# A decoder layer with a streamed mixture of experts: scratch memory shared with early constants, 8 MB of expert weights loaded ahead for items 10 to 13, finer last transfers, and the residual added in the accumulators

## The chip, the cores and the metric

The kernel runs on one core of one Trainium2 chip. The metric is the device time of one execution in microseconds (us), and the lower it is the better. The profile is that of one execution, and its times count from the first instruction of its span.

## The reference, cut to what matters

The layer takes 256 tokens of width 1024. It runs a sparse attention and an RWKV time mixing side by side, then a cross-attention into 256 memory tokens, and last a mixture of 32 experts of which every token takes four. The change lies in the mixture and in the way from the layers before it into it:

```
h = h + concat(o_nsa, o_rwkv) @ w_out
h = h + memory_cross_attention(rms_norm(h), rms_norm(mem), ...)
# mixture of experts on xt = rms_norm(h)
top_v, top_i = top_k(xt @ router_w + router_b, 4);  gate = softmax(top_v)
for every expert e, on the tokens that chose it:
    hb = xt[tok] @ mlp1_w[e] + mlp1_b[e]              # 1024 -> 2048
    hg = min(hb[::2], 7);  hl = clip(hb[1::2], -7, 7)
    yb = (hg * sigmoid(1.702 * hg) * (hl + 1)) @ mlp2_w[e] + mlp2_b[e]
    y[tok] += gate * yb
return h + y
```

All of it is float32. One expert's weights are 128 partitions x 24576 columns, which is 12 MB, and 32 experts have 384 MB. They are read once, so this stream is most of what the kernel moves.

## The kernel before

**Stages.** The kernel first runs the mixers and the cross-attention (called the front here, up to about 430 us of the trace), with a small ring of three weight slots (`wsl`, 1 MB each) that SyncE's queue fills in the order of `JOBS`. Then the router picks the experts, and the mixture runs in **items**: an item is one expert with up to 64 of its tokens. Items 0 to 31 are the experts in order; more would follow if an expert had more tokens than 64, and with these inputs there are none. Items are worked in pairs, of which `item(j, par)` is one; each pair gathers the tokens of both of its experts once.

**An item on TensorE.** `item` in the tensor block does, in this order: the first bias (L922), the first half of the first matrix (`hidden`, n=0, L909), two transposes (L927), its second half (L909), the transposes of the activations (L942), between them the scatter of the item before (`scatter`, L891: it adds gated results into four PSUM banks that stay open over all items), in odd items the gather for the next pair (`gather`, L882), and last the second matrix (L963). VectorE makes the clamps and products (L1455 to L1462) and ScalarE the sigmoid and the copies out of PSUM (L1498).

**Where the weights lie.** The buffer `ring` holds exactly one item: 24576 columns in six **pieces** of 4096 columns, 2 MB each. Pieces 0 to 3 are the first matrix, 4 and 5 the second. TensorE waits for `piece_in_c` ahead of a piece and counts `piece_used` up when it is through with one. SyncE's queue loads piece c of item i (`item`, `piece`, L1981) once piece c of the item that last used this part of the ring has been used:

```
def item(i, e, which=range(PIECES)):
    for c in which:
        sp.wait_ge(sem("piece_used"), i * PIECES + (c + 1 - PIECES))
        piece(e, c)
```

During the front the ring's memory belongs to the RWKV part. It comes free after that, and the six pieces of item 0 are loaded between the jobs of `w_out` and `xq_w`. In four more buffers that the front is through with (`ox`, `mixT`, `vx`, `qx`, 1 MB each) `piece_ahead` (L1992) puts pieces 0 and 1 of item 1. So at the start of the mixture 16 MB lie ready. The queue then goes on in this order: pieces 0 and 1 of item 2 (once item 0 has used them), pieces 2 to 5 of item 1, pieces 2 to 5 of item 2, and from item 3 on piece by piece.

```
for c in range(W1_PIECES):
    sp.wait_ge(sem("piece_used"), c + 1)
    piece(2, c)
item(1, 1, range(W1_PIECES, PIECES))
item(2, 2, range(W1_PIECES, PIECES))
```

**The scratch of the mixture** (clamps, products, selection matrices, biases, `yb`) lies in `wsl`, and the router's tables in `kxT`. So these 3 MB and 1 MB can't hold weights. Some 14 KB a partition of constants and small buffers (masks, vector rows, `dist`, `sc_c`, `xsq`, `xrs` and others) have their own memory, though only the front reads them.

**The end.** After the last item ScalarE copies `yb` out of PSUM in one piece, the last scatter (L891) runs, then VectorE adds the four open banks to the residual `h` (L1486, four instructions one after the other), and SyncE writes each of the four blocks out as it comes (L2028).

## Time and profile before

| | |
|---|---|
| time, median of 3 runs | 1368.34 us (1367.66 to 1369.61) |
| time of the profiled execution | 1367.88 us |
| its span, first to last instruction | 1366.1 us |
| TensorE busy (matmul) | 1258.0 us, 92% |
| VectorE, ScalarE, GpSimd busy | 352.2, 191.9, 43.5 us |
| read from memory | 440.72 MB, mean 323 GB/s over the span |
| mean granted clock of TensorE | 0.982 |

The profiled execution's time is its span and 1.8 us around it. PE stands for TensorE's matmuls, PEld for its weight loads (which overlap them), DVE for VectorE, ACT for ScalarE, SPq for the queue of SyncE, which issues nearly all transfers. A float32 matmul call shows as two records. Pieces of a chain or a timeline are merged groups of instructions with the start and the length of the group. The releaser behind an arrow is what ended a wait.

### The profile page before, as it was taken

Reading aid. Unit: us, or ns where it says so; the run is one execution under the profiler, and the core shown is the slowest. Engines: PE = TensorE matmul, PEld = TensorE weight load, DVE = VectorE, ACT = ScalarE, POOL = GpSimd, SP = SyncE. Lnnn points to the kernel's source line nnn. Section 1 sums busy time; section 2 is a strip of 40 time slices with the busy share of each in tenths; the row PEclk is TensorE's granted clock in tenths of the full one; section 3 lists DMA queues with packets and bytes.
Section 4 is the critical chain, followed back from the end, with each engine's and each line's share of the span. In section 5 each row is a group of like instructions: output and inputs, shape, how many; then the busy total and the mean of one; then the engine's idle time right before and its main releaser. Section 6 shows DMA issues by size and latency. Waiting matters only on the chain.

```text
span 1366.1 us, 19352 instructions
## 1 busy us (share of the span) xinstructions
PE 1258.0 (92%) x7798; PEld 645.7 (47%) x7798; DVE 352.2 (26%) x843; ACT 191.9 (14%) x457; POOL 43.5 (3%) x98
## 2 busy tenths in 40 slices
PE   7999889879898999999989989899998989989897
PEld 6888777758786333333332323333233332323332
DVE  3364642331224421121211212111111211212111
ACT  2242234411231000000000000000000000000000
POOL 7100001100000000000000000000000000000000
PEclk9999989999998999999999999999999999999999
DMA  7454111119631999999999999999999999999996
GB/s 237 124 113 137 64 63 32 33 32 377 238 133 38 384 385 429 428 429 429 427 429 427 429 429 428 428 429 427 429 429 428 428 428 428 429 429 428 428 427 281
DMA packets 75835, 442.44 MB, mean 324 GB/s; under 512 B 18720, under 2 KB 49550, under 8 KB 50958
## 3 DMA queue, kind: packets, MB, share of 16 engines
q1 hardware_dynamic: 75630, 441.26, 79.1%
q8 instruction: 34, 0.56, 0.2%
q0 software_dynamic: 160, 0.52, 0.1%
q14 instruction: 11, 0.09, 0.0%
HBM read 440.72 MB, written 1.05 MB: 323 GB/s over the span
## 4 chain that ended last, share of the span: by engine, by line
DMA 47%; PE 46%; DVE 4%; ACT 1%; issue 1%; POOL 0%; SPq 0%; DVEq 0%; ACTq 0%
DMA sb_ring<-in_mlp_w 47%; PE ps L909 14%; PE ps L359 9%; PE ps L687 6%; PE ps L963 4%; PE ps L558 2%; PE ps L882 1%; PE ps L891 1%; PE ps L720 1%; PE ps L410 1%; PE ps L816 1%; PE ps L922 1%; PE ps L428 1%; ACT sb_ring L1498 1%; DVE sb_qx L1002 0%
## 5 line engine op out<-in xcount | busy, mean ns | idle before, releaser
L909 PE MATMUL ps<-sb_ring,sb_hnT 128*64 128x512 f32 x2016 | 454.9, 598 | 50.3 <-DMA sb_ring<-in_mlp_w 48.8
L909 PEld LDWEIGHTS ps<-sb_ring,sb_hnT 128*64 128x64 f32 x2016 | 135.8, 137 | 346.1 <-issue 247.9
L963 PE MATMUL ps<-sb_ring,sb_hnT 128*64 128x512 f32 x1024 | 229.5, 596 | 0.0
L1455 DVE TENSOR_SCALAR sb_wsl<-ps 128x256 f32<-128x256 f32 x64 | 27.2, 425 | 659.1 <-PE ps L909 659.1
L963 PEld LDWEIGHTS ps<-sb_ring,sb_hnT 128*64 128x64 f32 x1024 | 72.2, 137 | 133.8 <-issue 132.0
L1498 ACT ACTIVATE sb_wsl<-sb_wsl 128x256 f32<-128x256 f32 x64 | 26.6, 416 | 528.2 <-DVE sb_wsl L1455 528.2
L359 PE MATMUL ps<-sb_hnT,sb_wsl 128*128 128x256 f32 x448 | 98.7, 380 | 1.7 <-DVE sb_hnT L1016 0.9
L359 PEld LDWEIGHTS ps<-sb_hnT,sb_wsl 128*128 128x128 f32 x448 | 84.9, 190 | 14.0 <-DVE sb_hnT L1016 1.3
L891 PE MATMUL ps<-sb_wsl 64*128 64x512 f32 x256 | 63.6, 615 | 0.7 <-ACT sb_wsl L1498 0.7
L882 PE MATMUL ps<-sb_wsl,sb_h 128*128 128x128 f32 x512 | 61.7, 281 | 1.6 <-DVE sb_wsl L1338 1.6
L882 PEld LDWEIGHTS ps<-sb_wsl,sb_h 128*128 128x128 f32 x512 | 60.3, 197 | 1.8 <-DVE sb_wsl L1338 1.8
L1498 ACT ACTIVATE sb_wsl<-ps 128x512 f32<-128x512 f32 (+1 forms) x33 | 19.5, 591 | 286.7 <-PE ps L963 268.8
L1498 ACT ACTIVATE sb_hnT<-ps 128x256 f32<-128x256 f32 (+1 forms) x80 | 31.8, 397 | 50.1 <-PE ps L942 47.5
L1430 DVE TENSOR_TENSOR sb_hnT<-ps,sb_vecs 128x512 f32<-128x512 f32 x32 | 20.6, 686 | 69.9 <-PE ps L882 69.9
L942 PEld LDWEIGHTS ps<-sb_ident,sb_hnT 128*128 128x128 f32 x128 | 12.9, 140 | 50.6 <-issue 26.0
L922 PE MATMUL ps<-sb_wsl,sb_hot 32*64 32x512 f32 x256 | 34.8, 613 | 1.4 <-DVE sb_hnT L1430 1.4
L891 PEld LDWEIGHTS ps<-sb_wsl 64*128 64x128 f32 x256 | 22.0, 186 | 21.8 <-issue 20.3
L687 PE MATMUL ps<-sb_wsl,sb_mixT 128*128 128x256 f32 x128 | 28.9, 385 | 1.4 <-DVE sb_mixT L1212 1.4
L687 PE MATMUL ps<-sb_wsl,sb_ox 128*128 128x256 f32 x128 | 29.6, 391 | 0.0
L558 PE MATMUL ps<-sb_ring 64*64 64x64 f32 x768 | 27.9, 234 | 1.8 <-DVE sb_ring L1155 1.3
L687 PE MATMUL ps<-sb_wsl,sb_qx 128*128 128x256 f32 x128 | 28.6, 382 | 0.5 <-ACT sb_qx L1498 0.5
L359 PE MATMUL ps<-sb_ox,sb_wsl 128*128 128x256 f32 x128 | 28.4, 380 | 0.0
(347 smaller groups left out, 965.8 us busy)
## 6 DMA issues: line engine op xcount, KB each, us to landing
sb_ring<-in_mlp_w SPq DMA_DIRECT2D x190, 2048.0 KB, 24.1
sb_wsl<-in_w_in SPq DMA_DIRECT2D x10, 1024.0 KB, 5.9
sb_wsl<-in_xk_w SPq DMA_DIRECT2D x4, 1024.0 KB, 5.1
sb_wsl<-in_xv_w SPq DMA_DIRECT2D x4, 1024.0 KB, 5.3
sb_wsl<-in_xq_w SPq DMA_DIRECT2D x4, 1024.0 KB, 10.3
sb_wsl<-in_xo_w SPq DMA_DIRECT2D x4, 1024.0 KB, 5.2
sb_wsl<-in_w_in SPq DMA_DIRECT2D x8, 256.0 KB, 4.2
sb_wsl<-in_w_out SPq DMA_DIRECT2D x8, 256.0 KB, 4.1
```

Of the source, the lines that this page charges most:

```text
L359: mm = pe.matmul(t[:, g * T:(g + 1) * T], w[:, k, g * P:(g + 1) * P], act[:, k, :], start=k == 0, stop=k == KD - 1)
L410: mm = pe.matmul(t[64 * par:64 * par + 64, b * P:(b + 1) * P], w[:, k, 64 * b:64 * b + 64], hnT[:, k, par:T:2], start=k == 0, stop=k == KD ...
L558: mm = pe.matmul(t[r, n * CH:(n + 1) * CH], BUF[lhs][r, m, :], moving, start=True, stop=True)
L687: mm = pe.matmul(t[:, tt * T:(tt + 1) * T], lhs(k, tt), w[:, k, :], start=k == 0, stop=k == KD - 1)
L882: mm = pe.matmul(psum[:, 4 + k // 4, k % 4 * PAIR:(k % 4 + 1) * PAIR], h[:, tt, k * P:(k + 1) * P], sel[:, tt, :], start=tt == 0, stop=tt ...
L891: mm = pe.matmul(psum[:, 2 * tt + o2, :], selgT[par][r, tt, :], yb[r, :], start=False, stop=False, skip_group_check=True)
L909: mm = pe.matmul(psum[64 * half:64 * half + 64, 4 + n, :], xgT[:, k, SLOTS * par:SLOTS * par + SLOTS], w[:, at + 512 * half:at + 512 * hal ...
L922: pe.matmul(psum[64 * half:64 * half + 64, 4 + n, :], hot[r, :], bias1[r, :], start=True, stop=False)
L963: mm = pe.matmul(psum[64 * o2:64 * o2 + 64, 7, :], actT[:, 2 * n + m, 64 * q:64 * q + 64], ring[:, at + 512 * o2:at + 512 * o2 + 512], sta ...
L1430: dve.tensor_tensor(xgT[:, 4 * n:4 * n + 4, :], view(psum[:, 4 + n, :], 0, 4, PAIR), bcast(g, P, 4, PAIR), ALU.mult).then_inc(sem("slots_i ...
L1455: dve.tensor_scalar(gl[:, n, :], psum[:, 4 + n, 0:256], 7.0, None, ALU.min).then_inc(sem("glu"), 1)
L1498: return act.activation(o, x, func, **kw)
```

## The change

- The constants and buffers of the front that had their own memory move into one buffer `early`, and the scratch and the tables of the mixture take that same buffer once the front is through. The halves of an item (n = 0, 1) now share one set of `gl`, `ll`, `sg`, and VectorE waits for its own last product ahead of writing them again. `bias1` goes to `hn`, the unread output of the squares (`junk`) to `xrs`.
- So `wsl` and `kxT` can take weights: eight buffers of 1 MB are loaded ahead, two for each of four items. They hold piece 0 of items 10, 11, 12 and 13 (before: pieces 0 and 1 of item 1). The two into `wsl` and the one into `qx` wait for the last jobs of `xo_w`.
- The queue's order in the mixture becomes plain: every piece (i, c) follows on the use of (i-1, c). Piece 0 of item 1 comes in two halves of 1 MB, of which the first waits only for the first half of item 0's piece (`half_used`). In items 10 to 13 the queue skips piece 0, and it adds the four missing increments to `piece_in_0` by hand. TensorE's loop is split into items 2 to 9, four items written out, and items 14 to 29.
- The last piece of the last item comes as 1 MB, 0.5 MB and 0.5 MB.
- After item 13 TensorE adds `h` into the four open banks with four matmuls by the identity. At the end ScalarE copies `yb` in two halves of 256 columns, the last scatter runs in two sides, and the four blocks go from PSUM to `h` by copies: two on VectorE, two on ScalarE.
- The table gets two more entries (index of the last item and of the one before it).

```diff
-        masks4 = sb("masks4", 4, CH)
-        dist = sb("dist", T)
-        sc_c = sb("sc_c", TT, 8, 16)
...
+        early = sb("early", 3680)
...
+        aheads = [(view(ox, 0, 2048), mixT[:, :, :].rearrange("p a b -> p (a b)")), (view(vx, 0, 2048), kxT[:, :, :].rearrange("p a b -> p (a b)")),
+                  (view(wsl, 2048, 2048), view(wsl, 4096, 2048)), (view(qx, 0, 2048), view(wsl, 0, 2048))]
+        AHEAD_AT = 10
...
                     if 1024 * (k + 1) % PIECE == 0:
                         mm.then_inc(sem("piece_used"), 1)
+                    elif stage == 0 and n == 0 and k == 1:
+                        mm.then_inc(sem("half_used"), 1)
...
+                            if last and par and n and q:
+                                pe.wait_ge(sem(f"late_in_{m}"), 16)
...
+            for a in range(4):
+                item((AHEAD_AT + a) // 2, a % 2, 1, ahead=a)
+                for bank in range(4) if a == 3 else ():
+                    pe.matmul(psum[:, bank, :], ident[:, :], h[:, bank // 2, bank % 2 * 512:bank % 2 * 512 + 512],
+                              start=False, stop=False, skip_group_check=True)
...
-            pe.wait_ge(sem("y_out"), last_pair * 2 + 3)
-            scatter(1)
+            for side in range(2):
+                pe.wait_ge(sem("y_out"), last_pair * 2 + 3 + side)
+                cols = slice(256 * side, 256 * side + 256)
+                for tt in range(TT):
+                    for o2 in range(2):
+                        r = slice(64 * o2, 64 * o2 + 64)
+                        mm = pe.matmul(psum[:, 2 * tt + o2, cols], selgT[1][r, tt, :], yb[r, cols],
+                                       start=False, stop=False, skip_group_check=True)
+                    if side:
+                        mm.then_inc(sem("scattered"), 1)
...
+                    dve.wait_ge(sem("swiglu"), i * 2 + 1 + n)
...
-            dve.wait_ge(sem("scattered"), last_pair * 2 + 2)
             for tt in range(TT):
-                for o2 in range(2):
-                    cols = h[:, tt, o2 * 512:(o2 + 1) * 512]
-                    link(dve.tensor_tensor(cols, psum[:, 2 * tt + o2, :], cols, ALU.add), "out_ready")
+                dve.wait_ge(sem("scattered"), last_pair * 2 + 2 + tt)
+                dve.tensor_copy(h[:, tt, 0:512], psum[:, 2 * tt, :]).then_inc(sem("out_left"), 1)
...
+            for tt in range(TT):
+                act.wait_ge(sem("scattered"), last_item + 1 + tt)
+                f(h[:, tt, 512:1024], psum[:, 2 * tt + 1, :], ACT.Copy).then_inc(sem("out_right"), 1)
...
+            def piece_ahead(n, half):
+
+                last_use = {(0, 0): ("wout", 3), (2, 0): ("xout", 1), (2, 1): ("xout", 2), (3, 0): ("xout", 3)}
+                if (n, half) == (1, 0):
                     sp.wait_ge(sem("ox"), 8)
+                elif (n, half) in last_use:
+                    sp.wait_ge(sem("tile_ready"), tiles[last_use[n, half]][1] + 1)
+                lo = 2048 * half
+                sp.dma_start(aheads[n][half], a["mlp_w"][AHEAD_AT + n, :, lo:lo + 2048]) \
+                  .then_inc(sem(f"ahead_in_{n}"), 16)
...
-            for c in range(W1_PIECES):
-                sp.wait_ge(sem("piece_used"), c + 1)
-                piece(2, c)
-            item(1, 1, range(W1_PIECES, PIECES))
-            item(2, 2, range(W1_PIECES, PIECES))
-
-            with sp.Fori(3, NE - 1) as i:
+            sp.wait_ge(sem("half_used"), 1)
+            piece(1, 0, at=(0, PIECE // 2))
+            sp.wait_ge(sem("piece_used"), 1)
+            piece(1, 0, at=(PIECE // 2, PIECE))
+            item(1, 1, range(1, PIECES))
+            with sp.Fori(2, AHEAD_AT) as i:
+                item(i, i)
+            for i in range(AHEAD_AT, AHEAD_AT + 4):
+                item(i, i, range(1, PIECES))
+            sp.sem_inc(sem("piece_in_0"), 16 * 4)
+            piece(AHEAD_AT + 4, 0)
+            item(AHEAD_AT + 4, AHEAD_AT + 4, range(1, PIECES))
+            with sp.Fori(AHEAD_AT + 5, NE - 2) as i:
                 item(i, i)
...
+            for c in range(PIECES - 1):
+                sp.wait_ge(sem("piece_used"), before_last * PIECES + (c + 1))
+                piece(e, c)
+            sp.wait_ge(sem("piece_used"), before_last * PIECES + PIECES)
+            piece(e, PIECES - 1, at=(24576 - 4096, 24576 - 2048))
+            piece(e, PIECES - 1, at=(24576 - 2048, 24576 - 1024), name="late_in_0")
+            piece(e, PIECES - 1, at=(24576 - 1024, 24576), name="late_in_1")
```

## Rows read from the trace of the kernel before

**Rows 1.** The page: 40 equal slices of the span, DMA busy tenths and GB/s.

```profile
DMA  7454111119631999999999999999999999999996
GB/s 237 124 113 137 64 63 32 33 32 377 238 133 38 384 385 429 428 429 429 427 429 427 429 429 428 428 429 427 429 429 428 428 428 428 429 429 428 428 427 281
```

**Rows 2.** The chain that ended last, in order of time: start, length, what.

```profile
600.68 7.02 PE ps L909 x32
608.06 7.04 PE ps L909 x32
615.26 24.29 DMA sb_ring<-in_mlp_w
639.60 3.68 PE ps L909 x16
643.43 25.49 DMA sb_ring<-in_mlp_w
...
1319.03 25.49 DMA sb_ring<-in_mlp_w
1344.57 3.65 PE ps L909 x16
```

**Rows 3.** Timeline of TensorE in items 3 to 5: start, length, operation.

```profile
538.81 7.09 PE L963 MATMUL ps<-sb_ring,sb_hnT 128*64 128x512 f32 x32
545.83 1.09 PE L922 MATMUL ps<-sb_wsl,sb_hot 32*64 32x512 f32 x8
...
592.57 7.09 PE L963 MATMUL ps<-sb_ring,sb_hnT 128*64 128x512 f32 x32
```

**Rows 4.** Stretches: start:end, us, busy of each engine, granted clock, DMA share, GB/s.

```profile
445.00:465.00 20.00, 19.66 (x100) 6.34 (x98) 12.83 (x35) 2.36 (x6) 0.00 (x0) 1.00 0.98 419
465.00:497.00 32.00, 32.00 (x168) 12.82 (x166) 6.48 (x18) 2.08 (x5) 0.00 (x0) 1.00 0.85 346
497.00:615.00 118.00, 118.00 (x586) 42.96 (x582) 23.19 (x65) 8.75 (x21) 0.00 (x0) 1.00 1.01 428
560.00:1000.00 440.00, 413.52 (x2030) 149.13 (x2027) 80.39 (x227) 32.34 (x78) 0.00 (x0) 1.00 1.01 428
```

**Rows 5.** Timeline of TensorE in items 0 and 1, where the ring's parts come free.

```profile
439.55 7.09 PE L909 MATMUL ps<-sb_ring,sb_hnT 128*64 128x512 f32 x32
...
471.80 7.09 PE L909 MATMUL ps<-sb_ring,sb_hnT 128*64 128x512 f32 x32
...
481.39 3.74 PE L882 MATMUL ps<-sb_wsl,sb_h 128*128 128x128 f32 x32
485.05 7.09 PE L963 MATMUL ps<-sb_ring,sb_hnT 128*64 128x512 f32 x32
```

**Rows 6.** Timeline of SyncE's queue before the mixture and at its start.

```profile
397.73 0.58 SPq L1992 DMA_DIRECT2D sb_ox<-in_mlp_w  x1
398.35 0.43 SPq L1992 DMA_DIRECT2D sb_mixT<-in_mlp_w  x1
398.82 0.52 SPq L1992 DMA_DIRECT2D sb_vx<-in_mlp_w  x1
420.39 0.33 SPq L1992 DMA_DIRECT2D sb_qx<-in_mlp_w  x1
443.24 172.35 SPq L1981 DMA_DIRECT2D sb_ring<-in_mlp_w  x38
```

**Rows 7.** DMA issues: count, KB each, median us from issue to landing.

```profile
sb_ox<-in_mlp_w SPq DMA_DIRECT2D x1, 1024.0 KB, 7.8
sb_mixT<-in_mlp_w SPq DMA_DIRECT2D x1, 1024.0 KB, 9.6
sb_vx<-in_mlp_w SPq DMA_DIRECT2D x1, 1024.0 KB, 11.8
```

**Rows 8.** Line 1981: issue to landing of the ring's transfers, shortest, median, longest.

```profile
DMA to landing us min/median/max: 7.2/24.1/25.5
```

**Rows 9.** The chain: one matmul call of 128x512 by a 128x128 matrix.

```profile
106.70 0.86 PE ps L446 x2
```

**Rows 10.** Timeline of the end, all engines.

```profile
1350.81 7.26 PE L963 MATMUL ps<-sb_ring,sb_hnT 128*64 128x512 f32 x32
...
1350.91 0.38 ACT L1498 ACTIVATE sb_hnT<-ps 128x256 f32<-128x256 f32 x1 [1.50 <-PE ps L942]
...
1358.10 0.60 ACT L1498 ACTIVATE sb_wsl<-ps 128x512 f32<-128x512 f32 x1 [6.80 <-PE ps L963]
...
1358.75 1.99 PE L891 MATMUL ps<-sb_wsl 64*128 64x512 f32 x8 [0.69 <-ACT sb_wsl L1498]
...
1360.78 2.87 DVE L1486 TENSOR_TENSOR sb_h<-ps,sb_h 128x512 f32<-128x512 f32 x4 [10.68 <-PE ps L891]
1361.50 2.51 SPq L2028 DMA_DIRECT2D out_h<-sb_h  x4
```

More of the change, by code:

```diff
@@ L893, in scatter, with landed, hidden @@
                 mm.then_inc(sem("scattered"), 1)
-            def hidden(i, par, n, first, second):
+            def landed(i, c, stage):
+                loads = i + 1 if c or stage == 0 else i + 2
+                pe.wait_ge(sem(f"piece_in_{c}"), loads * 16)
+            def hidden(i, par, n, stage, ahead):
                 for k in range(KD):
@@ L899, in hidden @@
                     c = at // PIECE
[L900 to L903 removed]
+                    if c == 0 and ahead is not None:
+                        if k == 0:
+                            pe.wait_ge(sem(f"ahead_in_{ahead}"), 32)
+                        w, at = aheads[ahead][k // 2], at % 2048
                     else:
                         if at % PIECE == 0:
[L906 removed]
+                            landed(i, c, stage)
                         w = ring
@@ L913, in hidden, with item @@
                         mm.then_inc(sem("piece_used"), 1)
-            def item(j, par, first=False, second=False, last=False):
+                    elif stage == 0 and n == 0 and k == 1:
+                        mm.then_inc(sem("half_used"), 1)
+            def item(j, par, stage, ahead=None, last=False):
                 i = j * 2 + par
+                first = stage == 0
                 pe.wait_ge(sem("slots_in"), j * 2 + 2)
@@ L922, in item @@
                     pe.matmul(psum[64 * half:64 * half + 64, 4 + n, :], hot[r, :], bias1[r, :], start=True, stop=False)
-                hidden(i, par, 0, first, second)
+                hidden(i, par, 0, stage, ahead)
                 pe.wait_ge(sem("gated"), i + 1)
@@ L934, in item @@
                     mm.then_inc(sem("gate_turned"), 1)
-                hidden(i, par, 1, first, second)
+                hidden(i, par, 1, stage, ahead)
                 if first:
@@ L2000, in _ @@
                     piece(0, left.pop(0))
-            for c in range(4):
-                piece_ahead(c)
+            for n in range(4):
+                for half in range(2):
+                    piece_ahead(n, half)
             def item(i, e, which=range(PIECES)):
```

114 lines of the change are left out of this document (50 added, 64 removed).

## The prediction

> **What bounds the kernel now.** I read the page's slices first. DMA stands at nine tenths and 427 to 429 GB/s from slice 16 on, with two slices of 384 and 385 just ahead and nearly nothing (38) before those [rows 1]: the mixture is a stream of weights, and it doesn't start at full rate. Next the chain that ended last. Up to 615 us it runs through TensorE's own matmuls; from there to the last item it is the ring's DMA, 25.49 us at a time with 3.68 us of L909 between [rows 2]. From 643.43 to 1319.03 are 23 items, so an item takes 29.37 us. How fast would TensorE be alone? In the timeline the second matrix starts at 538.81 and, two items later, at 592.57 [rows 3]: 26.88 us an item. So TensorE has 2.49 us an item to spare, and everything from item 7 on is paced by bytes: 12.58 MB in 29.37 us are 428 GB/s, which is what the stretch shows [rows 4], and a piece of 2 MB takes 4.895 us.
>
> The question is then: when does the stream start, when does it stand still, how many pieces go through it, and what follows the last one.
>
> **The change, term by term.**
>
> (1) **Fewer pieces in the stream.** Of 32 x 6 = 192 pieces the old kernel has 6 + 2 loaded before the stream starts, the new one 6 + 4. So 182 pieces go through in place of 184: 2 x 4.895 = 9.8 us. The Trainium skill, "HBM Reference" and "DMA: Bandwidth & Descriptors" (Specifications), gives some 358 GB/s as what one core gets from memory; by it the same 4.19 MB would be worth 11.7 us. The trace disagrees with it (428), and the sum takes 9.8.
>
> For that the added 4 MB must load in idle time. The last buffers of the new kernel come free when the old one's last did, at 420.39 [rows 6], and two transfers start there in place of one: by 4.895 us for 2 MB and the 2.3 us that the shortest landing has beyond its piece (7.2 - 4.9) [rows 8] they are in by 427.6, while the stream starts at 441. The others are released before that, between the first and the last of these rows. Ahead of them in the queue only the last `xo_w` job could suffer, and it is issued first. The two bias transfers on GpSimd's queue share the engines with at most 5 MB, 12 us, and they have 24. I count nothing.
>
> (2) **The two standstills.** After the first 8 of its pieces the old stream asks for the parts that item 1 is just using: piece (2,2) needs item 1's third piece used (471.80 + 3.5 = 475.3), and it would be due at 443.2 + 6 x 4.895 = 472.6; piece (2,4) needs the fifth used (485.05 + 3.5 = 488.6, behind scatter and gather) [rows 5] and is due some 3.4 us before. That is 2.7 + 3.4 = 6.1. The stretch 465 to 497 says the same: 346 for 428 GB/s over 32 us are 6.1 us lost [rows 4]. In the new order the n-th piece only needs the n-th use, two uses less: (2,2) is due at 481 and free at 475.3, (2,4) due at 490.8 and free at 488.6. Both standstills go: 6.1 us. One small one comes: (1,1) is due at 441.5 + 4.9 = 446.4 and free at 439.55 + 7.02 = 446.6, with its issue 0.3 us late. Net 5.8.
>
> (3) **An earlier start.** The first half of piece 0 is used after 8 of 32 records (1.76 us) in place of 16 (3.51) [rows 5], so the stream starts at 441.5 in place of 443.24 [rows 6]: 1.7 us. The second half's release at 443.2 comes before the first half is through (443.9).
>
> (4) **Is the gain kept?** Pieces left out in items 10 to 13 only help if the stream never stands still for a full ring. In these items it needs 5 x 4.895 = 24.5 us where TensorE needs 26.88, so it runs ahead: relative to the locked state it gains 4 x 4.895 = 19.6 us, TensorE 4 x 2.49 = 10.0, less the residual's matmuls. These are 4 calls of 0.86 us [rows 9], 3.4 us. So after item 13 the stream is 13.0 us further ahead than in the locked state. What room is there? A ring transfer now lands 24.1 us after its issue and could in 7.2 [rows 8], so it is issued 16.9 us before it can start. 16.9 - 13.0 leaves 3.9, of which the uneven items (odd ones with 3.66 us of gather [rows 5]) take most: laid out piece by piece, the tightest place is the second piece of item 13, with about 1 us. It holds. From item 14 TensorE catches up 2.5 us an item and by item 19 it waits for DMA again, with 12 items to go; so the whole gain arrives at the end, and the 3.4 us of the residual's matmuls cost nothing, since TensorE waits for the stream later anyway. If that cover were gone, they would cost 3.4.
>
> (5) **The rest of an item.** VectorE's added wait is on its own last product, long done: nothing queues behind it. Bound 0 to 32 x 2 x 0.1 us, beside matmuls. Taken as 0. The two added small instructions of the table lie under item 0.
>
> (6) **Finer last pieces.** The last wait for DMA ends at 1344.57, and a piece lands each 4.895 us: the fifth at 1349.5, the sixth at 1354.4. TensorE comes to the second matrix at 1350.81 and to its second half 3.57 us later, at 1354.38 [rows 10]: just when the sixth piece is in. It never waits there, so landing parts of it sooner gives nothing; upper bound 2.7 us (3 of the 4 quarters of 3.6 us), lower bound a loss if small transfers are slow. I take 0. The nearest rows for the latter are three 1 MB transfers issued together, which landed at 405.5, 407.95 and 410.6 [rows 6, 7]: 2.4 and 2.7 us apart, against 2.45 by the rate. So halves travel at full rate.
>
> (7) **The end.** Old: L963 ends at 1358.07, copy 0.60, scatter 1.99, then four adds in a row of 0.72 each, and the last output is issued at 1363.7 [rows 10], 5.6 us after L963. New: a half copy of 0.38 (as ScalarE's 128x256 copies [rows 10]), two sides of scatter of 1.0 each (half the columns; up to 1.5 if the weight loads set their pace), so the first two banks are ready at 2.0 and the last at 2.5. VectorE's two copies of 0.7 end at 2.7 and 3.5, ScalarE's in 2.6 and 3.3, and the queue issues at 2.8, 3.1, 3.5 and 3.8. Against 5.6 that is 1.8 us.
>
> **Sum:** 9.8 + 5.8 + 1.7 + 0 + 0 + 1.8 = 19.1 us. The profiled execution took 1367.9, so 1348.8; its time lies 0.5 us under the median of the runs, so against the median 1349.2.
>
> **Rivals.**
>
> A. **The ring fills.** The 1 us of room in item 13 comes from a model laid on one trace. If TensorE is slower in the four written-out items, or the residual's matmuls take more than 3.4 us, every us over the room is lost from the stream. 3 us lost: 1352.2. For it: the small room. Against: the layout gives the old kernel's last wait within 0.8 us (1343.8 for 1344.57). 10%.
>
> B. **Every added transfer costs the stream something fixed.** There are three more (one more in front, two more at the end). The Trainium skill, "DMA: Bandwidth & Descriptors" (Anatomy of one DMA and Measured), gives about 2 us fixed for each DMA and asks for at least 1 MB; the last two are half of that. As a mechanism here: the gap between two landings would be 2.45 + 2 us for a half piece, and 6 us would go from the gain, 1355.2. Against it stand the 2.4 and 2.7 us between the 1 MB landings [rows 6, 7]. 4%.
>
> C. **The finer end pays after all**, if the stream and not TensorE ends last there: up to 2.7 us more, 1346.5. 4%.
>
> D. **The change doesn't do what it says:** the added 4 MB delay the start of the mixture, so that (1) is paid in front. Then 9.8 us fall away: 1359.0. 1%.
>
> E. **Slower: TensorE's clock.** In items 10 to 18 TensorE would run for some 250 us without a wait, beside a full stream. If the granted clock fell to 1.2 GHz there, an item would take up to 2 x 26.9 = 53.8 us against the stream's 29.4: 24 us lost with each, less the room that the ring has at that place (1 us in item 13, some 5 later). So one item at that level takes the whole gain of 19, and two give 1349 + 48 - 5 = 1392. Against it: 497 to 615 is such a stretch, without a wait, DMA at 428, and the clock stands at 1.00 [rows 4]. 3%.
>
> **How the numbers follow.** The forecast's own case has 78%, 1347.5 to 1351, from the tail's scatter (1.0 to 1.5 a side), the extra standstill and the runs' own scatter of about 1 us. The range reaches to A and C: 1346.5 to 1352.8. A measurement of this kernel can tell 0.2%, 2.7 us, from no change. Faster by more than that: all but E and a rest, 96%; within it 1%; slower 3%.
>
> **What would show it.** (1, 2) Slices of 428 GB/s from the second slice of the mixture on, no stretch of 346; 182 pieces through the ring after item 0's six. (3) The first ring issue at about 441.5. (4) TensorE without DMA waits in items 10 to 18, the chain back on the DMA after that, and the last wait of L909 at about 1327 in place of 1344.57. (6) The last 32 records of L963 still in 7.2 us. (7) The last output issued 3.8 us after L963. Wrong it would be if a stretch near 780 to 880 us shows less than 428 GB/s (A), or the clock under 1.00 (E).

## The result, and the profile after

The changed kernel takes 1355.08 us (median of 4 runs, 1351.77 to 1356.38), the kernel before 1368.0 us beside it (4 runs, 1367.23 to 1369.61). The ratio is 0.99 with a 95% interval of 0.988 to 0.992. It is 1% faster, though by 12.9 us and not by 19.1, and 1355.1 lies above the range that the prediction gave.

The page of the changed kernel, its slices and parts that answer to [rows 1]:

```profile
span 1353.4 us, 19305 instructions
PE 1260.2 (93%) x7814; PEld 650.8 (48%) x7814; DVE 351.1 (26%) x843; ACT 193.0 (14%) x460; POOL 43.1 (3%) x98
DMA  7354211118715899999999999999999999999996
GB/s 240 125 109 138 70 64 32 33 33 322 292 64 240 343 427 429 427 429 428 429 428 428 428 415 428 427 429 430 427 429 430 428 428 429 429 427 430 429 427 284
q8 instruction: 41, 0.67, 0.2%
L904 PE MATMUL ps<-sb_ring,sb_hnT 128*64 128x512 f32 x1984 | 445.4, 597 | 34.9 <-DMA sb_ring<-in_mlp_w 33.8
```

The fifteenth slice, which had 385 GB/s, has 427 now; the stream starts in the fourteenth. The slice with 415 is new. The hidden matmuls wait 33.8 us in all for the ring; so the stream still ends an item where it ends one.

Its chain, in order of time (start, length, what), against [rows 2]:

```profile
564.02 23.00 DMA sb_ring<-in_mlp_w
587.07 3.68 PE ps L904 x16
...
704.57 3.65 PE ps L904 x16
...
829.00 3.63 PE ps L983 x8
...
955.76 23.19 DMA sb_ring<-in_mlp_w
978.99 3.68 PE ps L904 x16
...
1302.02 3.68 PE ps L904 x16
1305.85 26.82 DMA sb_ring<-in_mlp_w
1332.72 3.65 PE ps L904 x16
```

The chain is on the DMA from item 5 on (the wait that ends at 587.07; before from item 7 on), leaves it at item 9 (704.57), and comes back at item 19 (978.99). The residual's four matmuls (L983, 3.63 us) lie in that gap. One entry doesn't fit the pattern: the last DMA piece lasts 26.82 us, and those between 978.99 and 1302.02 last 25.5. Its reason is a good part of the answer.

The stretches that answer to [rows 4] (start:end, us, busy of PE, PEld, DVE, ACT, POOL, granted clock, DMA share, GB/s):

```profile
445.00:465.00 20.00, 19.66 (x98) 6.60 (x96) 13.72 (x32) 1.76 (x5) 0.00 (x0) 1.00 1.00 390
465.00:497.00 32.00, 32.00 (x172) 12.60 (x170) 8.28 (x28) 2.68 (x6) 0.00 (x0) 1.00 1.01 430
710.00:950.00 240.00, 240.00 (x1200) 90.22 (x1198) 46.99 (x135) 18.08 (x43) 0.00 (x0) 1.00 1.01 426
770.00:800.00 30.00, 30.00 (x144) 9.61 (x140) 5.18 (x17) 2.09 (x5) 0.00 (x0) 1.00 1.00 413
1302.00:1332.00 30.00, 25.90 (x118) 8.06 (x118) 4.23 (x12) 2.08 (x5) 0.00 (x0) 1.00 1.01 427
220.00:240.00 20.00, 19.80 (x145) 16.48 (x146) 4.48 (x8) 6.38 (x19) 2.04 (x2) 0.84 0.19 53
260.00:280.00 20.00, 17.39 (x371) 15.41 (x370) 5.27 (x13) 6.22 (x12) 1.89 (x1) 0.91 0.01 2
```

The standstills of 465 to 497 are gone (346 GB/s before, 430 now). The last two stretches are of the front, which the change hardly touches; in the kernel before they read so:

```profile
220.00:240.00 20.00, 19.19 (x149) 16.33 (x150) 4.49 (x8) 6.99 (x21) 2.65 (x2) 0.91 0.21 54
260.00:280.00 20.00, 17.39 (x374) 15.46 (x373) 5.27 (x13) 5.33 (x10) 1.89 (x1) 1.00 0.01 3
```

The granted clock was 0.84 and 0.91 where it had been 0.91 and 1.00 (1.00 is the level of 2.4 GHz, and the mean falls with every us spent at 1.2 GHz). Each of these two stretches made this execution about 1.5 us later against the kernel before, and by item 0 it was 2.5 us late:

```profile
442.07 7.09 PE L904 MATMUL ps<-sb_ring,sb_hnT 128*64 128x512 f32 x32
...
1302.02 3.65 PE L904 MATMUL ps<-sb_ring,sb_hnT 128*64 128x512 f32 x16 [0.49 <-DMA sb_ring<-in_mlp_w]
1308.26 3.65 PE L963 MATMUL ps<-sb_ring,sb_hnT 128*64 128x512 f32 x16
1313.23 3.65 PE L963 MATMUL ps<-sb_ring,sb_hnT 128*64 128x512 f32 x16 [1.31 <-DMA sb_ring<-in_mlp_w]
```

(Timeline of TensorE; item 0 begins at 442.07 where it was 439.55 [rows 5].) So I divide each span at two places that every kernel has: the start of item 0's first hidden matmul, and the end of the last L963. Between them is the **stream part**, behind it the **tail**.

| | item 0 | stream part | tail | span |
|---|---|---|---|---|
| before | 439.55 | 918.51 | 8.08 | 1366.1 |
| changed | 442.07 | 903.98 | 7.32 | 1353.4 |

The stream part gained 14.5 (forecast 9.8 + 5.8 + 1.7 = 17.3), the tail 0.8 (forecast 1.8), and the front lost 2.5, of which nothing was forecast. Three questions follow: is the front's loss the change's, which term of the stream is short, and why is the tail.

### The profile page after: what moved, and what is told of

It is laid out like the page before. It is cut to its first block, busy times and chain, and to the rows that moved or that the text cites. A ratio compares the mean times of both kernels' runs of the same rounds, so it can differ in the third digit from the quotient of the medians.

```text
span 1353.4 us, 19305 instructions
## 1 busy us (share of the span) xinstructions
PE 1260.2 (93%) x7814; PEld 650.8 (48%) x7814; DVE 351.1 (26%) x843; ACT 193.0 (14%) x460; POOL 43.1 (3%) x98
## 3 DMA queue, kind: packets, MB, share of 16 engines
HBM read 440.72 MB, written 1.05 MB: 326 GB/s over the span
## 4 chain that ended last, share of the span: by engine, by line
PE 59%; DMA 34%; DVE 4%; ACT 1%; issue 1%; POOL 0%; SPq 0%; DVEq 0%; ACTq 0%
DMA sb_ring<-in_mlp_w 34%; PE ps L904 19%; PE ps L349 9%; PE ps L963 7%; PE ps L677 6%; PE ps L872 2%; PE ps L548 2%; PE ps L881 2%; PE ps L920 1%; PE ps L940 1%; PE ps L710 1%; PE ps L400 1%; PE ps L418 1%; DVE sb_qx L1018 1%; ACT sb_ring L1515 1%
## 5 line engine op out<-in xcount | busy, mean ns | idle before, releaser
L904 PE MATMUL ps<-sb_ring,sb_hnT 128*64 128x512 f32 x1984 | 445.4, 597 | 34.9 <-DMA sb_ring<-in_mlp_w 33.8
L904 PEld LDWEIGHTS ps<-sb_ring,sb_hnT 128*64 128x64 f32 x1984 | 134.8, 137 | 321.3 <-issue 253.5
L963 PE MATMUL ps<-sb_ring,sb_hnT 128*64 128x512 f32 x1024 | 228.5, 596 | 1.3 <-DMA sb_ring<-in_mlp_w 1.3
L1474 DVE TENSOR_SCALAR sb_early<-ps 128x256 f32<-128x256 f32 x64 | 27.2, 425 | 645.5 <-PE ps L904 645.4
L963 PEld LDWEIGHTS ps<-sb_ring,sb_hnT 128*64 128x64 f32 x1024 | 71.7, 137 | 134.6 <-issue 132.8
L1515 ACT ACTIVATE sb_early<-sb_early 128x256 f32<-128x256 f32 (+2 forms) x72 | 29.4, 409 | 526.5 <-DVE sb_early L1474 516.0
L1515 ACT ACTIVATE sb_early<-ps 128x512 f32<-128x512 f32 (+4 forms) x44 | 23.0, 525 | 292.0 <-PE ps L963 269.1
L872 PE MATMUL ps<-sb_early,sb_h 128*128 128x128 f32 x512 | 61.8, 281 | 1.6 <-DVE sb_early L1354 1.6
L881 PE MATMUL ps<-sb_early 64*128 64x512 f32 x248 | 61.6, 615 | 0.0
L872 PEld LDWEIGHTS ps<-sb_early,sb_h 128*128 128x128 f32 x512 | 60.3, 197 | 1.8 <-DVE sb_early L1354 1.8
L940 PEld LDWEIGHTS ps<-sb_ident,sb_hnT 128*128 128x128 f32 x128 | 12.9, 141 | 50.6 <-issue 26.0
L920 PE MATMUL ps<-sb_hn,sb_hot 32*64 32x512 f32 x256 | 34.8, 613 | 1.4 <-DVE sb_hnT L1448 1.4
L881 PEld LDWEIGHTS ps<-sb_early 64*128 64x128 f32 x248 | 21.4, 186 | 19.8 <-issue 19.8
```

The lines of the kernel that those rows point to most:

```text
L872: mm = pe.matmul(psum[:, 4 + k // 4, k % 4 * PAIR:(k % 4 + 1) * PAIR], h[:, tt, k * P:(k + 1) * P], sel[:, tt, :], start=tt == 0, stop=tt ...
L881: mm = pe.matmul(psum[:, 2 * tt + o2, :], selgT[par][r, tt, :], yb[r, :], start=False, stop=False, skip_group_check=True)
L904: mm = pe.matmul(psum[64 * half:64 * half + 64, 4 + n, :], xgT[:, k, SLOTS * par:SLOTS * par + SLOTS], w[:, at + 512 * half:at + 512 * hal ...
L920: pe.matmul(psum[64 * half:64 * half + 64, 4 + n, :], hot[r, :], bias1[r, :], start=True, stop=False)
L940: mm = pe.transpose(psum[:, 6, m * P:(m + 1) * P], actv[:, m * P:(m + 1) * P], ident[:, :])
L963: mm = pe.matmul(psum[64 * o2:64 * o2 + 64, 7, :], actT[:, 2 * n + m, 64 * q:64 * q + 64], ring[:, at + 512 * o2:at + 512 * o2 + 512], sta ...
```

## The experiments

Each kernel was timed against the kernel before on its own chip. The parts of a span (item 0, stream part, tail) are each read from one profiled execution of a kernel.

**repeat** is the changed kernel once more, with no edit.

> The changed kernel once more, nothing edited. In its first profile item 0's first matmul starts 2.5 us later than before (442.07 against 439.55), in two places of the front where the granted clock was lower. Theory 1, the clock's dips fall by chance: the start of item 0 lies between 439.5 and 442.5 and differs from the first profile, single times spread from 1351 to 1357. Theory 2, the change itself delays the front (moved buffers): item 0 starts at 442.0 to 442.2 again and all times lie within 1 us. Either way the median is 1353 to 1356.

Measured: 1353.78 us (6 runs, 1349.88 to 1356.78) beside 1369.26 for before; ratio 0.9883 [0.9862, 0.9903]. Item 0 at 441.71, stream part 903.46, tail 7.33. The stream part repeats within 0.5 us. The runs scatter by 7 us, also those of the kernel before (17 runs, 1365.64 to 1372.36).

**before_a, before_b** are the kernel before again, one execution each, for the scatter of its parts.

> The kernel before once more, for a second profile. So far its only profile has item 0's first matmul at 439.55 us, and nine profiles of kernels with the moved buffers have it at 438.1 to 442.1, 440.6 in the mean. Theory, the granted clock in the front falls by chance and the buffers have no part in it: item 0 starts anywhere between 438 and 442.5, and the part from there to the end of the last L963 is 918 to 919 us. Rival, the moved buffers cost the front 1 us: the kernel before starts at 439.3 to 439.7 again.

> The kernel before a third time, for the same: item 0's start between 438 and 442.5 by the theory of chance, 439.3 to 439.7 by the rival; the part from item 0 to the end of the last L963 918 to 919 us.

Item 0 in the timelines of TensorE, first of one, then of the other:

```profile
441.88 5.37 PE L909 MATMUL ps<-sb_ring,sb_hnT 128*64 128x512 f32 x24
```

```profile
438.84 7.09 PE L909 MATMUL ps<-sb_ring,sb_hnT 128*64 128x512 f32 x32
```

The same kernel comes to item 0 at 438.84, 439.55 or 441.88, while its stream part is 918.58, 918.51 and 918.09 and its tail 8.08, 8.08 and 8.09. All kernels of this study came there between 438.08 and 442.07. So the 2.5 us in front lie within the 3.0 us by which the kernel before scatters there, while its stream part scatters by 0.5 and its tail by 0.01. Like with like, the change gives 918.4 - 903.7 = 14.7 us in the stream and 8.08 - 7.32 = 0.76 in the tail, 15.5 in all. The medians beside repeat differ by 1369.26 - 1353.78 = 15.5 too; their interval reaches from 13 to 19, so that they agree to the tenth is luck.

The clock is not all of the front's scatter. Over 0 to 438 us repeat and the kernel before have the same mean granted clock, 0.95, and yet repeat comes to item 0 2.2 us later. It has these 2.2 us by 23 us, ahead of any fall of the clock: a copy of VectorE (`sb_vecs`, 128x74) starts at 22.77 there and at 20.77 in the kernel before. What delays it stays open.

**old_order** keeps the new memory layout and the new end, but loads the 4 MB of item 1 ahead and uses the old order of the queue. **two_ahead** has the new order and loads 4 MB ahead too, for items 10 and 11. Between them lie the order and the place of the 4 MB (terms 2 and 3), between two_ahead and the changed kernel the bytes (term 1).

```diff
 # old_order
-sp.wait_ge(sem("half_used"), 1); piece(1, 0, at=(0, PIECE // 2)); ...
+for c in range(W1_PIECES):
+    sp.wait_ge(sem("piece_used"), c + 1)
+    piece(2, c)
+item(1, 1, range(W1_PIECES, PIECES)); item(2, 2, range(W1_PIECES, PIECES))
 # two_ahead
-for a in range(4):
+for a in range(2):
```

> The changed kernel with the old order of the stream: 4 MB ahead, used as pieces 0 and 1 of item 1, pieces 0 and 1 of item 2 next, no early half. What is left of the change is its end (residual by TensorE, halves, copies on two engines, finer last pieces). Forecast's term 7: 1.8 us faster than before, about 1366.2. From the first profile of the changed kernel (end after the last L963 7.35 us against 8.03): 0.7 us, about 1367.3. The two standstills of the stream (landing steps of 6.9 and 8.2 us in place of 4.9) must be back.

> The changed kernel with two items ahead in place of four (items 10 and 11, 4 MB, as many bytes as before). Theory: each 2 MB piece ahead is worth 4.9 us, so 9.8 us slower than the changed kernel, about 1364.5, and 2.5 to 3.5 us faster than the old order by 5.8 + 1.7 less what is lost at the stream's start; that would make old_order about 1371.5 - so if old_order is 1367, two_ahead should be 1367 - 7.5 = 1359.8 and the two readings can't both hold: which of them does tells whether the bytes or the order brought less than forecast. Rival, the ring fills in items 12 to 16 with four pieces ahead: two_ahead is less than 9 us slower than the changed kernel.

| | median us | ratio | stream part | tail |
|---|---|---|---|---|
| old_order | 1370.22 (12 runs) | 1.0003 [0.9989, 1.0017] | 917.97 | 7.95 |
| two_ahead | 1362.01 (6 runs) | 0.9952 [0.9935, 0.997] | 912.84 | 7.33 |
| repeat | 1353.78 (6 runs) | 0.9883 [0.9862, 0.9903] | 903.46 | 7.33 |

The stretch 465 to 497 of old_order:

```profile
465.00:497.00 32.00, 32.00 (x170) 12.67 (x164) 7.41 (x22) 2.60 (x6) 0.00 (x0) 1.00 0.84 345
```

With the old order the standstill is back (345 GB/s, [rows 4] has 346) and the whole gain is gone: layout, shared scratch and VectorE's added wait cost nothing that shows. The bytes bring 912.84 - 903.7 = 9.1 us (forecast 9.8). The order brings 917.97 - 912.84 = 5.1 (forecast 7.5). This second term is the short one.

Neither difference is as sharp as it looks. The two pieces more are worth their 9.8 us at 4.895 each. But two_ahead has its third ring transfer in 17.3 us after item 0's start, where the changed kernel has it at 15.7 and 15.4, and from there on it loses 1.1 us where the changed kernel loses 3.5. The two nearly cancel, 9.8 + 1.75 - 2.4 = 9.1. By the ledger below the order is worth some 4.6 us in the changed kernel. (The tail of old_order, 7.95, is another matter: its last write is issued at +4.51 behind the end of L963 instead of +4.18, and a fetch of 8 KB of instructions runs beside its writes.)

**Where it is short.** Each transfer leaves 16 landing marks in the trace, and TensorE is released by the last of them. In the changed kernel they read, around its two longest steps:

```
transfer   first mark   last mark   step of the last   spread
           525.21       526.94      4.89               1.73
           530.10       533.17      6.23               3.08
           534.99       538.07      4.89               3.08
...
           1304.78      1306.87     4.89               2.09
           1309.68      1313.09     6.22               3.41
           1314.58      1317.99     4.89               3.41
```

The first marks keep their 4.9 us. The last falls behind, by 1.3 us, and stays behind as long as the stream runs without a pause: the spread is 3.1 us up to 769 us. It falls to 2.1 near 780 to 800, where the ring is nearly full and the engines wait for a release, and from there it grows again. The DMA view of 1310 to 1312 (queue and kind: packets, MB, share of the engines) shows what else was there:

```profile
q1 hardware_dynamic: 61, 0.85, 101.5%
q8 instruction: 1, 0.02, 3.3%
```

One packet of 16 KB of instructions, 1.07 us long, at 1310.46, and one at 527.5 ahead of the other late step. The byte rate doesn't show it (427 in that stretch, above). The packets bear no engine number, but all sixteen marks of a piece do show that one engine carries the fetch. Here are the marks of the last pieces ahead of a fetch and behind it, in us after the first mark (the lower twelve are left out, they keep their places within 0.03):

```
fetch      ahead of it                behind it
527.50     1.50 1.58 1.71 1.73        1.48 1.69 1.73 3.08
1310.46    1.87 1.87 1.95 2.09        1.87 1.94 2.07 3.41
```

One mark leaves its place and comes back 1.5 us later (1.58 to 3.08, 1.87 to 3.41), and the other fifteen stay. So it is in all 14 traces of this study: of the 177 fetches of 16 KB from 452 us on, 157 move exactly one mark, by 1.4 to 2.0 us, 1.58 in the median. The other 20 fall beside a standstill, at the ring's tight place, together with another fetch or behind the last piece. The 1.58 are two parts: the fetch's own 1.07, and the packet of weights behind it, which takes 1.07 to 1.16 us where the others take 0.61 (in 135 of 136 fetches between 500 and 1330 us).

This also tells which fetches are seen. Every one delays its engine by some 1.6 us, but the piece lands later only by what that engine then lies behind the last of the others: at 1310.46 that is 3.41 - 2.09 = 1.32. The seven fetches from 721 to 879 us each moved a mark too, but one that had lain far enough ahead (0.39 to 2.0, 0.32 to 1.97 and so on), and cost 0 to 0.1 us each. The changed kernel's code sets how many fetches there are; on which engine each falls I can't read from the traces.

The marks also show what a standstill costs. Around the two in the kernel before:

```
transfer   first mark   last mark   step of the last   spread
           474.41       475.96      4.87               1.55
           482.25       482.84      6.88               0.59
           487.12       487.70      4.86               0.58
           495.49       495.93      8.23               0.44
           500.39       502.27      6.35               1.88
```

At the last mark the two cost 6.88 and 8.23 less 4.895 each, 5.3 us (4.9 in both repeats of this kernel, 5.0 in old_order), and not the 6.1 that the rate of all engines gave. All engines wait for the same release, and the late one, which has the least to wait, draws level: the spread falls from 1.55 to 0.44. The next fetch, at 496.72, opens it again, with 1.46 us.

Now the ledger, all at last marks. **Late steps** are what the steps behind a fetch take over 4.895 us, from the third transfer of the stream on, less what single steps are shorter.

| | standstills | third transfer in, from item 0 | released late | late steps | fetches behind 435 us |
|---|---|---|---|---|---|
| before, before_a, before_b | 5.3, 4.9, 4.9 | 16.9, 16.9, 16.9 | 0 | 1.6, 1.7, 2.1 | 7, 7, 7 |
| old_order | 5.0 | 16.9 | 0 | 1.5 | 11 |
| changed, repeat | 0 | 15.7, 15.4 | 0.53, 0.58 | 3.2, 3.0 | 15, 15 |

The third transfer is piece (1,1); in the kernel before and in old_order, where no piece is split, it is the second. Either way 4 MB of the stream are then in. With the means of before the forecast of 17.3 us goes over into the measured 14.7 so: standstills 5.05 for 6.1, -1.05; start 1.35 for 1.7, -0.35; one late release of 0.55 (at 463.18, piece (1,2)) for 0.3 at (1,1), -0.25; late steps 3.1 for 1.8, -1.3. That makes -2.95 for -2.6. Of the rest of 0.35 the finer last pieces gave 0.17 (below), and 0.2 is not assigned.

**unroll** adds fetches alone: TensorE's loop over items 2 to 9 and ten items of the later loop are written out.

```diff
-with pe.Fori(1, AHEAD_AT // 2) as j:
+for j in range(1, AHEAD_AT // 2):
...
+for j in range(AHEAD_AT // 2 + 2, AHEAD_AT // 2 + 7):
```

> The changed kernel with TensorE's items 2 to 9 and 14 to 23 written out in place of looped, nothing else: the same work, but some 30 more fetches of 16 KB of instructions while the stream runs. Theory A, a fetch holds one of the 16 DMA engines for about 1.1 us, and a piece lands with its slowest engine: time is lost only where the fetches of one engine add up beyond the others, 1 to 4 us slower than the changed kernel, with landing steps of up to 6.2 us just after fetches. Theory B, each fetch delays the whole stream: 30 x 1.1 = 33 us slower. Theory C, fetches cost nothing: the same within 1 us.

Measured: 1355.09 us (5 runs), ratio 0.9902 [0.9885, 0.992]; stream part 906.94, tail 7.32. Its page:

```profile
q8 instruction: 58, 0.95, 0.3%
```

17 more packets than in the changed kernel (41), all of them in the mixture (32 for 15), late steps of 6.4 us in place of 3.1 (the step into the third transfer, 0.3 late, is counted in), and a stream part 3.2 us longer than the mean of the changed kernel's two. Item 0 came at 438.08 in this execution, which is why its span isn't longer. The median hardly differs from the changed kernel's; it hides an effect of 3 us that the parts show.

**no_half**: the first half of item 1's piece 0 waits for the whole piece, as all others (term 3). **whole_last**: the last piece in one transfer of 2 MB (term 6).

```diff
 # no_half
-sp.wait_ge(sem("half_used"), 1)
-piece(1, 0, at=(0, PIECE // 2))
 sp.wait_ge(sem("piece_used"), 1)
+piece(1, 0, at=(0, PIECE // 2))
 # whole_last
-for c in range(PIECES - 1):
+for c in range(PIECES):
...
-piece(e, PIECES - 1, at=(24576 - 2048, 24576 - 1024), name="late_in_0")
...
```

> The changed kernel, but both halves of item 1's piece 0 wait for the whole piece 0 of item 0. Forecast's term 3: the stream starts 1.7 us later (first ring issue 3.7 us after item 0's first matmul in place of 2.0) and everything ends 1.7 us later. Rival, the first transfers of the stream are slowed by fetches and by the release of piece 1 anyway: the second landing lies only 0.5 to 1.2 us later, and so does the end. Medians move by less than their scatter of 2 to 3 us, so the landings of the profile decide.

> The changed kernel with the last piece of the last item in one transfer of 2 MB. Forecast's term 6: no difference, the last 32 records of L963 take 7.1 us without a wait in both. Rival C: up to 2.7 us slower, with a wait for DMA inside L963. Rival B: faster, since two fixed costs fall away.

no_half: 1354.02 us (6 runs), ratio 0.9882 [0.9861, 0.9902], stream part 903.46. whole_last: 1354.9 us (6 runs), ratio 0.9893 [0.9872, 0.9913], stream part 904.31. SyncE's queue from 440 to 450, first the changed kernel, then no_half:

```profile
444.05 5.48 SPq L2003 DMA_DIRECT2D sb_ring<-in_mlp_w  x3
```

```profile
445.57 3.76 SPq L2003 DMA_DIRECT2D sb_ring<-in_mlp_w  x3
```

Measured from item 0 the first issue is at +1.98 with the early half and at +3.69 without it: the forecast 1.7 us are there, and 1.2 to 1.5 of them at piece (1,1). Yet the stream part of no_half and of repeat is the same to 0.01 us. With the early half the stream then asks for piece (1,2) 0.5 us too soon, and repeat has 3.0 us of late steps where no_half has 1.5. Whether an early half always meets more late steps, so few executions can't say.

whole_last, the last 32 records of the second matrix:

```profile
1337.93 7.25 PE L961 MATMUL ps<-sb_ring,sb_hnT 128*64 128x512 f32 x32
```

They take 7.25 us, as in [rows 10] (7.26), and not the 7.09 that TensorE needs for them when everything is in ([rows 3], and the changed kernel's 1338.96 below). So the finer last pieces do bring something, but only these 0.17 us: in the three executions of the kernel before, in whole_last, fine_start and fine_unroll L963 ends 13.49 to 13.51 us after the last wait of L904 or L909, in the eight with finer pieces 13.32 or 13.33.

**at_2** uses the same 8 MB in items 2 to 5, a test of whether the place of the left-out pieces matters (terms 1 and 4).

```diff
-AHEAD_AT = 10
+AHEAD_AT = 2
...
```

> The changed kernel with the four pieces ahead used in items 2 to 5 in place of 10 to 13. The ring is nearly full there, so the stream should stand still: laid out piece by piece with the rates of the first profile it loses 9.2 us more, so some 1363. It would show that placement, not only bytes, makes the gain. In return the standstills should swallow the delays after fetches (spread of one piece's 16 landings back to 0.5 us or so), so 7 to 9 us slower than the changed kernel. Rival, TensorE's pace in those items leaves room: within 2 us of the changed kernel.

Measured: 1361.03 us (6 runs), ratio 0.9939 [0.9918, 0.996]; stream part 911.21, 7.5 us longer. Its stretches:

```profile
497.00:517.00 20.00, 20.00 (x96) 6.62 (x96) 4.22 (x12) 1.61 (x5) 0.00 (x0) 1.00 0.93 371
517.00:560.00 43.00, 43.00 (x222) 16.31 (x216) 8.34 (x23) 2.98 (x7) 0.00 (x0) 1.00 0.95 392
```

Here the ring is full and the queue waits for TensorE, which has no idle moment. In the changed kernel the same question is answered by the chain above: from the wait that ended at 704.57 to the one that ended at 978.99 lie ten items, 60 pieces less the 4 left out, 56 x 4.895 = 274.1 us, and 274.42 were measured. 0.3 us are lost. In the stretch 770 to 800 (413 GB/s, above) the ring does touch its limit, which is the sign that the prediction gave for rival A: the rate is short by 1.0 us, the last marks by 0.2, since there too the late engine waits least (the spread falls from 3.1 to 2.1).

**two_queues** lets ScalarE's queue issue the two right-hand output blocks, a test of whether the pace of the issues sets the tail.

```diff
+for tt in range(TT):
+    act.wait_ge(sem("out_right"), tt + 1)
+    act.dma_start(out[0, tt * P:(tt + 1) * P, 512:1024], h[:, tt, 512:1024]).then_inc(sem("out_done"), 16)
...
-    for o2 in range(2):
+    for o2 in range(1):
```

> The changed kernel with the right halves of the output issued by ScalarE's queue and the left ones by SyncE's. In the changed kernel the last of four issues starts 4.17 us after L963's end, three of them 0.41 to 0.49 us apart, and lands 2.72 us later. Theory, the queue's issue pace sets the end: the last issue starts 3.5 us after L963's end and the end comes 0.5 to 1.0 us sooner. Rival, the landings share something else: the same end within 0.2 us.

Measured: 1353.03 us (6 runs), ratio 0.988 [0.9857, 0.9903], tail 7.33. The end of the changed kernel, all engines, and then the two queues of this one:

```profile
1338.96 7.09 PE L963 MATMUL ps<-sb_ring,sb_hnT 128*64 128x512 f32 x32
...
1346.09 0.66 ACT L1515 ACTIVATE sb_early<-ps 128x256 f32<-128x256 f32 x2 [6.64 <-PE ps L963]
...
1346.53 2.00 PE L996 MATMUL ps<-sb_early 64*128 64x256 f32 x16 [0.48 <-ACT sb_early L1515]
1348.14 1.08 ACT L1515 ACTIVATE sb_h<-ps 128x512 f32<-128x512 f32 x2 [1.39 <-PE ps L996]
1348.14 1.29 DVE L1503 COPY sb_h<-ps 128x512 f32<-128x512 f32 x2 [9.79 <-PE ps L996]
1348.86 1.82 SPq L2066 DMA_DIRECT2D out_h<-sb_h  x4
```

```profile
1347.39 0.90 ACTq L1815 DMA_DIRECT2D out_h<-sb_h  x2
1347.48 0.94 SPq L2069 DMA_DIRECT2D out_h<-sb_h  x2
```

From L963's end the four issues come at +2.82, 3.22, 3.69 and 4.18 in the changed kernel and at +2.72, 2.82, 3.21 and 3.41 here. The last landing comes at +6.90 and +6.91. Issuing the last one 0.8 us sooner moves nothing. The reason stands in the DMA share of the stretch in which the four writes run, for the kernel before, the changed kernel and two_queues:

```profile
1362.35:1365.35 3.00, 0.00 (x0) 0.00 (x0) 1.27 (x2) 0.00 (x0) 0.00 (x0) 0.74 0.94 350
1349.70:1352.60 2.90, 0.00 (x0) 0.00 (x0) 0.00 (x0) 0.00 (x0) 0.00 (x0) 1.00 0.97 362
1348.30:1351.20 2.90, 0.00 (x0) 0.00 (x0) 0.00 (x0) 0.00 (x0) 0.00 (x0) 0.71 0.98 362
```

In all three the DMA engines are busy for 94 to 98% from the first packet to the last, 2.9 to 3.0 us for 1 MB. So the end is the first write's start and 2.9 us behind it, and the pace of the later issues doesn't matter as long as it keeps the engines fed. The first issue comes at +2.82 where it came at +3.44 in the kernel before, 0.6 us sooner, and with the 0.1 us that the writes themselves are shorter this is the tail's gain of 0.76.

**fine_start** carries the early start to its end: item 1's piece 0 comes in 0.5, 0.5 and 1 MB, pieces 1 to 3 in halves, each as soon as its own columns are used. The last piece is whole.

```diff
-piece(1, 0, at=(0, PIECE // 2))
+piece(1, 0, at=(0, PIECE // 4))
+sp.wait_ge(sem("half_used"), 2)
+piece(1, 0, at=(PIECE // 4, PIECE // 2))
...
+for c in range(1, 4):
+    sp.wait_ge(sem("half_used"), c + 2)
+    piece(1, c, at=(PIECE * c, PIECE * c + PIECE // 2))
+    sp.wait_ge(sem("piece_used"), c + 1)
+    piece(1, c, at=(PIECE * c + PIECE // 2, PIECE * c + PIECE))
```

> The changed kernel with item 1's first piece in 0.5, 0.5 and 1 MB and its pieces 1 to 3 in halves of 1 MB, each part waiting only for its own columns of item 0, and the last piece of the last item whole. The stream can start 0.9 us earlier (first ring issue 1.1 us after item 0's first matmul in place of 2.0) and the late third piece of the stream (0.6 us) goes: from item 0's start to the end of the last L963 902.2 us in place of 903.7, 1.5 us faster than the changed kernel, 1352.5. Rival, as in the run without the early half: what the start wins is given back at the next fetch, 903.5 us and no difference.

Measured: 1351.13 us (4 runs, 1349.89 to 1352.21) beside 1367.32; ratio 0.9872 [0.985, 0.9894]; stream part 901.99. (TensorE's counts of used halves change with it.) Its queue and first stretch:

```profile
442.25 6.34 SPq L2001 DMA_DIRECT2D sb_ring<-in_mlp_w  x5
```

```profile
445.00:465.00 20.00, 19.66 (x99) 6.44 (x95) 13.55 (x36) 1.76 (x5) 0.00 (x0) 1.00 1.02 413
```

The stream starts at +1.12, the late release at 463 is gone, and late steps are 2.0 us. It is the shortest stream part of all, 1.5 and 2.0 us under the two of the changed kernel. How much of that is the start, and how much a kinder fall of the fetches, one execution can't tell: the late steps alone differ by 1.0 to 1.2 us. Against the changed kernel the ratios' intervals overlap, so as a time this isn't settled. Its ratio is the lowest of the study, but not clear of the others.

**fine_unroll** puts the two together, with TensorE's items 2 to 9 and 14 to 27 written out on fine_start (edits as above).

> The kernel of fine_start with TensorE's items 2 to 9 and 14 to 27 written out in place of looped: the same work and the same transfers of weights, but some 36 fetches of 16 KB of instructions while the stream runs in place of 15. Theory A (a fetch holds one DMA engine, and what an engine loses beyond the others is never made good): late landings after fetches, from item 0 to the end of the last L963 904 to 907 us in place of 902.0, so 2 to 5 us slower than fine_start. Theory B, each fetch delays the whole stream by its 1.1 us: 925. Theory C, the 3 us of the first written-out kernel were chance: 902.0 to 902.8.

Measured: 1355.48 us (6 runs), ratio 0.9906 [0.9888, 0.9924]; stream part 906.24, tail 7.32. 36 fetches in the mixture, late steps of 6.3 us in place of 2.0, stream part 4.25 longer. Its page:

```profile
q8 instruction: 62, 1.02, 0.3%
```

With unroll that is twice that added fetches (17, then 21) came with added late steps (3.3, 4.3) and with as much more length of the stream (3.2, 4.25). Here too all but a few fetches, those where the ring is nearly full, moved one mark; the losses are the four steps in unroll (1.5 to 1.7 us each) and some fifteen in fine_unroll (0.1 to 1.2 each) where the moved mark overtook the last. A loss that goes by the number of pieces, or one by the clock, would have stayed away, since both are the same in each pair (mean granted clock 0.980 to 0.983 over the span).

## Why the prediction was wrong, step by step

- **(1) Fewer pieces: 9.8, measured 9.1.** Held; the 0.7 are fetches that fell otherwise. The rate was 427 to 430 GB/s, as read from [rows 4]. The prediction set it against 358 GB/s of the Trainium skill and said that the trace disagrees. That figure is the share of a core while its neighbour streams too; for a core that streams alone the same page ("HBM Reference", Specifications) gives about 425 GB/s, and with this the trace agrees.
- **(2) Standstills: this is the step that failed.** Both went, as forecast (430 for 346 GB/s). I priced them by the rate of all engines, "6.1 us lost", where the kernel waits for the last one, which loses 5.0. And the step took for granted that the stream then runs at 4.895 us a piece, a term for late landings that stood at nothing without a reason; 15 fetches add 3.1 us to it where 7 had added 1.8. The one late release that it forecast, 0.3 us at (1,1), came as 0.55 us at (1,2). With (3), the order brought 5.1 for 7.5. (Its "first 8 of its pieces" should read six, as its sum has it; the other two lie ahead.) The Trainium skill, "Runtime: NRT & Kernel Launch" (Instruction fetch mechanics), calls the cost of crossing a 16 KiB boundary "mostly hidden" and says that kernels prefer full unrolling. In the landings of this stream a fetch was worth up to 1.5 us, and 17 more made it 3.2 us longer; so here the trace disagrees.
- **(3) Earlier start: 1.7 at the issue, 1.2 to 1.5 at piece (1,1),** and nothing that the stream part of no_half can tell.
- **(4) Kept in the ring: held.** No wait of TensorE for DMA from 708 to 950 us, 0.3 us lost. The forecast room of about 1 us in the ring was not there, but the tightest place was, near 780 to 800 us. Rival A's sign came (413 GB/s there), but not its price: 0.2 us at the last marks for the 3 us it stood for. The mechanism is real, and at_2 shows it at 7.5 us. The residual's matmuls (3.63 us) cost nothing.
- **(5), (6): nothing forecast; nothing that shows (old_order) and 0.17 us (whole_last).** The reading behind (6), no wait in 7.26 us, was off by these 0.17. Rival C, up to 2.7 us, fell with it.
- **(7) The tail: 1.8, measured 0.76.** The last issue comes at +4.18, not +3.8, for the old +5.6. That is 1.4 us sooner, and half of it doesn't arrive: the last landing came sooner by 0.76 only. The step followed the last issue. What sets the end is the first one, 0.6 us sooner, and 2.9 us of full DMA engines behind it.
- **The front, 2.5 us in the profiled execution,** is no step of the change. My scatter "of about 1 us" was too narrow; single runs of the kernel before span 1365.5 to 1373.0. Without the front's 2.5 us, 15.5 us under the 1368.3 that the forecast started from would be 1352.8, just the upper end of the range. So what the first measurement lies beyond the range is bad luck in the front; that it comes near the range's end at all is (2) and (7).
- **Rivals B, D and E fell.** The 1 MB halves of fine_start land 2.45 to 2.49 us apart, but for one behind a fetch, so nothing fixed comes with each (the 2 us that the prediction took from the Trainium skill are given there for transfers that GpSimd issues, and mostly as time to completion); the last of the ahead loads was in at 430.1, and item 0's start is within the scatter of the kernel before; the clock stood at 1.00 from 710 to 950.

The sum as it came: 9.1 + 5.1 + 0.8 = 15.0, beside 15.5 by the parts, and 2.5 off by the front in the first profile. The last wait of L904 ended at 1332.7 and not at about 1327: 2.5 us of front and 2.6 of stream.

## What to carry to other kernels

Where a stream of transfers bounds a kernel, price its pauses by the last landing mark of each transfer and not by GB/s: a loss on one engine shows in the first alone, and a pause costs the late engine less than the others. In such a stream written-out code has a price, since each 16 KB of instructions holds back one of the sixteen engines by some 1.6 us, and once the engines ahead have used up their lead, the stream is later by it. And a change of this size is measured by parts of the span that repeat, rather than by medians.

## What the runs showed that I had not expected

A 16 KB instruction fetch takes about 1.07 us on one DMA engine, slows the packet behind it, and moves that engine's later landings by some 1.6 us and the piece's by up to 1.5. In the changed kernel the marks' spread goes from 0.4 to 3.1 us, back to 2.1 at the ring's tight place, and ends at 3.4; in fine_unroll it ends at 6.3. Of 15 fetches at most two cost over 1 us, and which ones differs: late steps are 1.5 us in no_half and 3.3 in whole_last, with 15 fetches each. A fetch shows when the engine that it holds lies less than 1.6 us ahead of the last; what decides which engine that is stays open. And the same kernel comes to item 0 with a scatter of 3 us. Two falls of the granted clock, worth 1.5 us each, make it in one case, and 2 us in the first 23 us, whose cause stays open, in another.
